# A fused attention, convolution, recurrence and expert layer: who splits the gate weights, and how the recurrence's output tiles are ordered

## What is computed

```python
n = rmsnorm(h, norm1_g) * (1 + sc1) + sh1
(qa, ka, va, u, gb, gc, qc, zf, zb, ic, oc, ga, gbr, gcr) = split(n @ w_in)
o_a = attention(qa, ka, va, cache, rpb)
o_b = gb * conv3(gc * u)
o_c, s_f, s_b = bidirectional_hgrn2(qc, zf, zb, ic, s0)   # f = lb + (1-lb) sigmoid(z)
o_c = rmsnorm_per_head(o_c) * hgrn_g * silu(oc)
mix = (sigmoid(ga) * (o_a @ w_br_a) + sigmoid(gbr) * (o_b @ w_br_b) + sigmoid(gcr) * (o_c @ w_br_c)) @ w_out
h = h + g1 * mix
h = h + g2 * moe(rmsnorm(h, norm2_g) * (1 + sc2) + sh2)   # 64 experts, top 8, and a shared one
y = rmsnorm(h, final_norm_g)
```

## Time and profile before

| | us |
|---|---|
| runs | 1250.66, 1258.70, 1261.13 (median 1258.7) |
| profiled execution, its own time | 1262.51 |
| its span | 1260.7 |
| PE busy | 1144.5 (91%) |
| PEld busy | 700.2 (56%) |
| DVE busy | 446.7 (35%) |
| ACT busy | 291.3 (23%) |
| POOL busy | 180.6 (14%) |

### The profile page before, as it was taken

One profiled execution on the slowest core, in us unless ns is written; L12 is line 12 of the kernel. 1 busy time (PEld: TensorE's weight loads), 2 busy tenths in 40 slices (PEclk: granted clock), 3 DMA queues, 4 the chain that ended last, 5 costly groups with the idle time before them and its releaser, 6 DMA issues.

```text
span 1260.7 us, 14771 instructions
## 1 busy us (share of the span) xinstructions
PE 1144.5 (91%) x4912; PEld 700.2 (56%) x4912; DVE 446.7 (35%) x949; ACT 291.3 (23%) x437; POOL 180.6 (14%) x163
## 2 busy tenths in 40 slices
PE   5999888899888896899987899999999999999965
PEld 2469777687778765556454444444444444444422
DVE  1033333633897835342452221212122121212116
ACT  3124333326434322200131211111111111111001
POOL 0200222000433300000000511112111111111100
PEclk9899898899999997898988999999999999999988
DMA  9845555255633312240046789999999999999464
GB/s 358 258 104 155 81 81 66 76 213 195 224 134 135 134 68 84 68 148 1 1 151 246 282 337 381 386 382 403 379 394 374 382 386 408 391 390 388 171 279 187
DMA packets 86115, 292.40 MB, mean 232 GB/s; under 512 B 10346, under 2 KB 14698, under 8 KB 70954
## 3 DMA queue, kind: packets, MB, share of 16 engines
q1 hardware_dynamic: 69440, 258.05, 53.0%
q0 software_dynamic: 12976, 27.29, 9.6%
q10 hardware_dynamic: 3652, 6.44, 1.5%
HBM read 284.79 MB, written 25.30 MB: 246 GB/s over the span
## 4 chain that ended last, share of the span: by engine, by line
PE 53%; DVE 4%; DMA 4%; ACT 1%; issue 1%; DVEq 0%; SPq 0%; POOL 0%; POOLq 0%
PE PS L1874 14%; PE PS L1530 12%; PE PS L1891 7%; PE PS L1876 7%; PE PS L1893 3%; PE PS L1860 3%; DMA y_parts<-bigB,IDX 2%; PE PS L1540 2%; PE PS L1941 1%; DMA bigA<-in_w_sh_down 1%; DMA nT<-n_rows,IDX 1%; PE PS L1909 1%; PE PS L1740 1%; PE PS L1747 0%; DMA bigA<-y_parts 0%
## 5 line engine op out<-in xcount | busy, mean ns | idle before, releaser
L1581 PE MATMUL PS<-bigB_r 128*128 128x384 f32 x288 | 98.9, 344 | 3.3 <-ACT bigD L743 1.3
L1874 PE MATMUL PS<-bigB 128*128 128x512 f32 x224 | 101.7, 597 | 0.0
L984 POOL DMA_INDIRECT bigB<-n_rows,IDX x29 | 30.0, 1034 | 496.1 <-DVE IDX L1057 249.3
L1583 PE MATMUL PS<-bigB_r,bigA_r 128*128 128x384 f32 x288 | 97.3, 338 | 0.0
L1582 PE MATMUL PS<-nT_r,bigB_r 128*128 128x384 f32 x288 | 97.2, 338 | 0.0
L1874 PE MATMUL PS<-bigA,bigB 128*128 128x512 f32 x208 | 94.9, 599 | 0.0
L1877 PE MATMUL PS<-bigB 128*64 128x512 f32 x208 | 94.8, 599 | 0.0
L1876 PE MATMUL PS<-bigA,bigB 128*64 128x512 f32 x208 | 94.8, 599 | 0.0
L1487 DVE TENSOR_SCALAR bigB<-PS,bigD 128x1024 f32<-128x1024 f32 x40 | 51.4, 1284 | 104.8 <-PE PS L1891 70.6
L1128 DVE TENSOR_TENSOR bigA_r<-bigA,bigB_r 128x2048 fp32r<-128x2048 f32 x18 | 41.3, 2292 | 116.5 <-ACT bigB_r L765 116.5
L907 ACT ACTIVATE bigB<-PS 128x1024 f32<-128x1024 f32 x40 | 41.0, 1024 | 153.3 <-PE PS L1860 149.1
(11 more groups left out here) (336 smaller groups left out, 2003.3 us busy)
## 6 DMA issues: line engine op xcount, KB each, us to landing
bigA<-in_w_in SPq DMA_DIRECT2D x17, 2048.0 KB, 9.1
bigB<-in_w_gate SPq DMA_DIRECT2D x27, 1024.0 KB, 10.5
bigB<-in_w_up SPq DMA_DIRECT2D x27, 1024.0 KB, 13.6
bigB<-in_w_down SPq DMA_DIRECT2D x27, 1024.0 KB
bigA<-in_w_gate SPq DMA_DIRECT2D x26, 1024.0 KB
bigA<-in_w_up SPq DMA_DIRECT2D x26, 1024.0 KB
bigA<-in_w_down SPq DMA_DIRECT2D x26, 1024.0 KB, 11.5
bigA<-in_w_ada SPq DMA_DIRECT2D x8, 2048.0 KB, 9.6
```

The source lines that it names most:

```text
L1581: mm(out, wh, nh, start=(k == 0), stop=False)
L1583: last = mm(out, wl, nh, start=False, stop=(k == KD - 1))
L1874: last = mm(PS[:, 2 + b, :], XT[:, b, k, :], GU_W[s][:, :, k, :], start=first, stop=stop)
```

## The change

GpSimd's low parts of the gate weights go to VectorE (low_part), issued one or two units ahead inside the stages sums and ops, and behind the carry keys for the last ones. All 24 gate units are rounded; n_back and its semaphore are gone. All gate units now stand ahead of carry_t. A new stage late_sig does the first sigmoid and the output gate's SiLU on ScalarE. The output tiles get a bank and a row buffer each (HO_BANK, OS[m]); their stages are split in ho_sq and ho_norm, and branch products 0 to 3 (br) with their gating (brm) are put among them; the other 20 follow. The decayed queries EB are computed in place of the running sums. The modulation rows of the second norm come back as columns, in two transfers (MODP) whose contiguous pieces have eight elements, and VectorE adds them up instead of TensorE's 32 matmuls. The gate bias is added ahead of branch product 8.

The new order of the tail is in the list below (context lines are cut, the indentation of the engine code is reduced by eight):

```diff
 PASSES = UNITS_MAX // BODY
+BR_EARLY = 4
+HO_BANK = (6, 4, 5)
...
-SPLIT_G = [n for n, (name, c, j) in enumerate(UNITS) if name[0] == "g" and name[1].isdigit()][:19]
+SPLIT_G = [n for n, (name, c, j) in enumerate(UNITS) if name[0] == "g" and name[1].isdigit()]
...
         s.append(("split_g", SPLIT_G[SPLIT_G.index(n) + 2]))
-    if n == SPLIT_G[-1]:
-        s.append(("n_back",))
...
     for i in range(16):
-        stages += [(("level", i), 0), (("ops", i + 1) if i < 15 else ("carry",), 1 if i < 15 else 2)]
-    stages += [(("carry_t",), 2), (("carry_products",), 2), (("hout", 0), 1), (("hout_t", 0), 1), (("hout", 1), 1),
-               (("hout_t", 1), 1), (("hout", 2), 1), (("hout_t", 2), 0)]
+        stages += [(("level", i), 0), (("ops", i + 1) if i < 15 else ("carry",), 1 if i < 15 else 5)]
...
         fill = fill[n:]
-    late = [("late_act", b) for b in range(3)]
-    while fill or late:
-        s += late[:1] + sum(fill[:1], [])
-        late, fill = late[1:], fill[1:]
+    assert not fill
+    s += [("carry_t",), ("late_sig",), ("carry_products",), ("br", 0), ("br", 1), ("hout", 0), ("brm", 0), ("brm", 1),
+          ("ho_sq", 0), ("ho_norm", 0), ("hout", 1), ("hout_t", 0), ("ho_sq", 1), ("ho_norm", 1), ("hout", 2), ("br", 2),
+          ("ho_sq", 2), ("ho_norm", 2), ("hout_t", 1), ("br", 3), ("brm", 2), ("hout_t", 2), ("brm", 3)]
+    s += [("late_act", b) for b in range(3)]
...
 XH = cut(bigB, ATT, (NT, D))
-T1 = bigB[:, ATT + 3072:ATT + 3584]
+T1 = OQ = bigB[:, ATT + 3072:ATT + 3584]
...
 GR = bigB[:, 20000:22048]
-Zrows = bigB[:, 22048:24096]
...
 PTC = bigC[:, 5632:5760]
-EB = cut(bigC, 0, (2, HC, 2 * P))
+EB = Z[:, :, :, CTX:T]
 STC = cut(bigC, 2048, (2, HC, P))
-OS, OQ, OR = bigC[:, 3072:3584], bigC[:, 3584:4096], bigC[:, 4096:4608]
+OS = [bigC[:, 3072 + 512 * m:3584 + 512 * m] for m in range(NT)]
+MODP = cut(bigC, 5632, (2, 4, 2 * KD))
...
 nlo_done = sem("n_low_ready")
-nback_done = sem("n_whole_again")
...
+def br_bank(i):
+    return (2, 3, 0, 1)[i % 4] if i < KD else (4, 5, 2, 3, 0, 1)[(i - KD) % 6]
...
             act.wait_ge(b_done, 1)
-            act.wait_ge(nback_done, KD)
             link(nc.scalar.activation(KH, KH, ACT.Exp))
-            nc.scalar.activation(EB, Z[:, :, :, CTX:T], ACT.Exp).then_inc(edec_done, 1)
+            nc.scalar.activation(EB, EB, ACT.Exp).then_inc(edec_done, 1)
...
                                      ACT.Copy).then_inc(kht_taken, 1)
+        elif st == "late_sig":
+            act.wait_ge(unit_taken, len(UNITS))
+            nc.scalar.activation(G[:, 0:8, :], G[:, 0:8, :], ACT.Sigmoid).then_inc(late_done, 1)
+            nc.scalar.activation(OG, OG, ACT.Silu).then_inc(late_done, 1)
...
             act.wait_ge(ho_ready, m + 1)
-            if m > 0:
-                act.wait_ge(ho_norm, m)
-            nc.scalar.activation(OS, PS[:, 6, :], ACT.Copy).then_inc(ho_taken, 1)
+            nc.scalar.activation(OS[m], PS[:, HO_BANK[m], :], ACT.Copy).then_inc(ho_taken, 1)
+            if m == 0:
+                for d in range(2):
+                    act.dma_start(new_state[d].rearrange("h k v -> k h v"), STC[:, d, :, :]).then_inc(state_out, 16)
+        elif st == "ho_norm":
+            m = ev[1]
...
             nc.scalar.activation(small[:, 36:40], small[:, 32:36], ACT.Sqrt).then_inc(ho_root, 1)
-            if m == 0:
-                act.wait_ge(unit_taken, AFTER["oc"])
-                nc.scalar.activation(OG, OG, ACT.Silu).then_inc(late_done, 1)
-                for d in range(2):
-                    act.dma_start(new_state[d].rearrange("h k v -> k h v"), STC[:, d, :, :]).then_inc(state_out, 16)
...
             if b == 0:
-                act.wait_ge(unit_taken, AFTER["g5"])
...
                 for g in range(P // CG):
-                    act.dma_start(bigB[CG * g:CG * g + 2, 20000:24096], ada_rows[g]).then_inc(ada_back, 16)
+                    act.dma_start(GR[CG * g:CG * g + 2, :], ada_rows[g, :, 0:4 * WCH]).then_inc(ada_back, 16)
+                for i in range(2):
+                    cols = ada_rows[:, :, (4 + 2 * i) * WCH:(6 + 2 * i) * WCH].rearrange("g v (p k) -> p (g v) k", k=KD)
+                    act.dma_start(MODP[:, i, :, :].rearrange("p g (v k) -> p (g v) k", v=2), cols).then_inc(ada_back, 16)
...
                 act.dma_start(BG[0:2, :], b_gate).then_inc(bg_loaded, 16)
-            g = G[:, 8 * b:8 * b + 8, :]
-            nc.scalar.activation(g, g, ACT.Sigmoid).then_inc(late_done, 1)
+            else:
+                g = G[:, 8 * b:8 * b + 8, :]
+                nc.scalar.activation(g, g, ACT.Sigmoid).then_inc(late_done, 1)
...
-    for n in SPLIT_G:
-        w, low, i = gate_unit(n)
-        pool.wait_ge(ghi_done, i + 1)
-        nc.gpsimd.tensor_tensor(low, w, GHI[i % 2].bitcast(F32), ALU.subtract).then_inc(glo_done, 1)
...
-    def mod_columns(which, ks, norm, cnt):
+    def mod_columns(which, ks, norm, cnt, src):
...
         n = ks.stop - ks.start
-        src = PS[:, 7, 0:32].rearrange("p (s k v) -> p s v k", s=2, v=2)
...
+    lows = []
...
+    def low_part():
...
+        w, low, i = gate_unit(lows.pop(0))
+        dve.wait_ge(ghi_done, i + 1)
+        nc.vector.tensor_tensor(low, w, GHI[i % 2].bitcast(F32), ALU.subtract).then_inc(glo_done, 1)
...
                 nc.vector.tensor_tensor(NLO[:, k, :], nT[:, k, :], NHI[:, k, :].bitcast(F32), ALU.subtract).then_inc(nlo_done, 1)
-        elif st == "n_back":
-            dve.wait_ge(nlo_done, KD)
-            dve.wait_ge(nmove_done, 1)
-            dve.wait_ge(unit_ready, SPLIT_G[-1] + 1)
-            for k in range(KD):
-                nc.vector.tensor_tensor(nT[:, k, :], NLO[:, k, :].bitcast(F32), NHI2[:, k, :].bitcast(F32), ALU.add).then_inc(nback_done, 1)
+        elif st == "split_g":
+            lows.append(ev[1])
+            if SPLIT_G.index(ev[1]) == 2 or SPLIT_G.index(ev[1]) > 20:
+                low_part()
...
             dve.wait_ge(modt_ready, hf + 1)
-            mod_columns(0, slice(4 * hf, 4 * hf + 4), cc(C_N1), hf + 1)
+            mod_columns(0, slice(4 * hf, 4 * hf + 4), cc(C_N1), hf + 1,
+                        PS[:, 7, 0:32].rearrange("p (s k v) -> p s v k", s=2, v=2))
...
         elif st == "sums":
+            low_part()
...
             for h in range(HC):
+                if h == 2:
+                    low_part()
...
                 take_level(i - 1)
+            else:
+                low_part()
+            low_part()
...
                     ins.then_inc(diff_done, 1)
+            low_part()
...
             dve.wait_ge(in_state, 32)
+            dve.wait_ge(unit_taken, len(UNITS))
...
             nc.vector.tensor_copy(small[:, 83:84], small[:, 56:57]).then_inc(st_done, 1)
-        elif st == "hout":
+        elif st == "ho_sq":
...
             dve.wait_ge(ho_taken, m + 1)
-            link(nc.vector.tensor_tensor(OQ, OS, OS, ALU.mult))
+            link(nc.vector.tensor_tensor(OQ, OS[m], OS[m], ALU.mult))
...
             nc.vector.tensor_scalar(small[:, 32:36], small[:, 40:44], 1.0 / P, EPS, ALU.mult, ALU.add).then_inc(ho_ms, 1)
+        elif st == "ho_norm":
+            m = ev[1]
...
             rsqrt_fix(small[:, 32:36], small[:, 36:40], small[:, 44:48], small[:, 88:92])
-            if m > 0:
-                dve.wait_ge(hot_ready, m)
-            nc.vector.tensor_tensor(OR.rearrange("p (h v) -> p h v", h=HC), OS.rearrange("p (h v) -> p h v", h=HC),
-                                    small[:, 44:48].unsqueeze(2).broadcast_to([P, HC, P]), ALU.mult).then_inc(ho_norm, 1)
+            rows = OS[m].rearrange("p (h v) -> p h v", h=HC)
+            nc.vector.tensor_tensor(rows, rows, small[:, 44:48].unsqueeze(2).broadcast_to([P, HC, P]), ALU.mult).then_inc(ho_norm, 1)
+            dve.wait_ge(ho_norm, m + 1)
+        elif st == "brm":
+            i = ev[1]
+            dve.wait_ge(late_done, 1)
+            dve.wait_ge(br_ready, i + 1)
+            nc.vector.tensor_tensor(G[:, i, :], PS[:, br_bank(i), 0:T], G[:, i, :], ALU.mult).then_inc(br_taken, 1)
...
             m = ev[1]
-            dve.wait_ge(late_done, 1)
+            dve.wait_ge(late_done, 2)
...
-            dve.wait_ge(unit_taken, len(UNITS))
-            dve.wait_ge(bg_loaded, 16)
-            dve.wait_ge(ada_back, 64)
-            nc.vector.tensor_tensor(GR[0:2, :], GR[0:2, :], BG[0:2, :], ALU.add).then_inc(gr_ready, 1)
-            for i in range(24):
+            for i in range(BR_EARLY, 24):
                 br, j = i // KD, i % KD
+                if i == KD:
+                    dve.wait_ge(bg_loaded, 16)
+                    dve.wait_ge(ada_back, 96)
+                    nc.vector.tensor_tensor(GR[0:2, :], GR[0:2, :], BG[0:2, :], ALU.add).then_inc(gr_ready, 1)
...
                     dve.wait_ge(late_done, 2 + br)
+                    dve.wait_ge(br_taken, i)
...
                 g = G[:, 8 * br + j, :]
-                nc.vector.tensor_tensor(g, PS[:, i % 6, 0:T], g, ALU.mult).then_inc(br_taken, 1)
```

(46 more changed lines are left out.)

## The result

The changed kernel takes **1220.0 us** (median of four runs, 1213.4 to 1221.3) where the kernel before takes 1254.8 on the same chip: a ratio of **0.971, 95% interval 0.965 to 0.977**. The profiled execution of after has a span of 1219.4 us and a time of 1221.25, for 1260.7 and 1262.51 before.

A forecast was written before the change was run, and what follows sets the result against it. VectorE, standing still behind GpSimd, was taken to pace the level steps. 12.4 - 3.7 + 10.2 + 13.4 + 9.1 = 41.4, less 2 allowance, gave 1223.1 us for the profiled execution, 1219 for the median; range 1209 to 1238.

The forecast's parts named there:

- The allowance of 2 us: TensorE idling 2.6 us ahead of the first transposes might halve its clock, costing 3 to 5; 2 us put in.
- The level steps: Low parts on VectorE: round 6.2 us instead of 7.59, level 15 at 433.7 instead of 446.07; gain 12.4 us.
- The five rounded units: Units 19 to 23 behind level 15, before the carry products: stage takes 29.0 us for 25.3; loss 3.7.
- Carry products to the first tile: VectorE's path from carry products to first output tile unchanged at 9.0 us; nothing gained, tile starts at 471.7.
- The 1.7 us that the prediction worked out by that rule: ScalarE before the first output tile: 1.38 us drain beside each table load would add some 1.7 us to the sum.
- The output tiles: Three tiles overlapped in the new order: 18.3 us for 28.5; gain 10.2, bounds 6 and 12.
- Branch products and gate rows: Behind the tiles: 20 branch products instead of 24 gain 13.4 us; modulation columns on VectorE and gate rows gain 9.1.
- The rival of late modulation rows: Two new transfers of 1024 32-byte pieces land late, stopping VectorE at branch product 8; 1271 us at 78 us, chance 0.03.
- the rival it belongs to: Half clock returns: idles at 475 and 487 drop TensorE's clock over tiles and branch products; 1225 us, chance 0.22.
- the 673.5 us behind: The stretch from the first output product (587.2) to the end is not touched by the change.

The follow-up runs named there:

- low_pool: The changed kernel with the low parts of all 24 rounded gate units subtracted on GpSimd again; median 1234.5 us, ratio 0.977 to the kernel before.
- low_only: The kernel before with only its 19 low parts moved to VectorE between the level steps; median 1243.0 us, ratio 0.986 to the kernel before.
- low_twice: The changed kernel with each low part of the level steps subtracted a second time on VectorE into a scratch; median 1233.9 us, ratio 0.978.
- eb_later: The changed kernel with the exponential of the output decays issued two rounded units later on ScalarE; median 1222.4 us, ratio 0.969.
- unround5: The changed kernel with the last five gate units unrounded again after re-adding the activations, all ahead of the carry transposes; median 1222.8 us, ratio 0.966.
- tiles_serial: The changed kernel with the three output tiles one after the other again, branch products 2 and 3 behind the last; median 1235.9 us, ratio 0.979.
- mod_pe: The changed kernel with the modulation columns made by 32 small TensorE products as before; median 1226.5 us, ratio 0.971.
- tiles_later: The changed kernel with a branch product ahead of each group of transposes and two more products moved in; median 1216.7 us, ratio 0.966.
- both_later: The changed kernel with the later output-decay exponential and branch products 2 to 5 among the output tiles; median 1208.9 us, ratio 0.961.
- before_again: The kernel before, unchanged, run for a second profile; one run, 1269.2 us.

## Why the prediction was right

The forecast was 1219 us; the median is 1220.0. The mechanism was right. That the number agrees within 1 us is luck: the steps of the sum gave 45.7 us where it had 41.4, and 39.4 after the allowance; nearly all of that error has one sign, and it was made up for behind the first output product (7). The median of before was 1258.7 when the forecast was made and 1254.8 with the fourth run, so the medians differ by 34.8 us only.

1. **The level steps** gained 14.8 where I had 12.4. The mechanism stands (low_pool, low_only, low_twice). The round was 5.96 for my 6.2: I took the overlap of successive instructions off the differences alone (1.9), and durations for the masks and the low part (1.06 and 1.2), while the rows have 0.96 and 1.13 from start to start. Twelve steps by 0.24 are 2.9, most of the error. The steps with an adaLN unit went as foreseen: one of them and the step behind it take 13.35 us for 13.5.
2. **The five rounded units** lost 2.8 where I had 3.7. I had the waits at 1.2 and 2.1, on units 20 and 21; they were 0.93 and 1.99. The second was there for a cause that I named (two exponentials) but took as given, and eb_later took it away. The rest of the error is behind the units, where transposes and copies took 2.3 for 2.9. Rounding these five is worth 2.0 (unround5).
3. **Carry products to the first tile** took 9.05, as foreseen, with two table loads on ScalarE. This is its timeline there:

```profile
459.08 1.08 ACT L828 ACTIVATE bigB<-PS 128x512 f32<-128x512 f32 x2 [0.32 <-PE PS L1715]
460.18 1.28 ACT L832 ACT_TABLE_LOAD   x1
461.48 2.76 ACT L832 ACTIVATE bigB<-bigB 128x3072 f32<-128x3072 f32 x1
464.26 1.28 ACT L833 ACT_TABLE_LOAD   x1
465.55 1.49 ACT L833 ACTIVATE bigD<-bigD 128x1536 f32<-128x1536 f32 x1
```

Each load of 1.28 us starts within 0.02 of the end of the activation ahead of it, and the next activation starts 0.02 behind. The Trainium skill, ScalarE: Activation LUTs, What ACT_TABLE_LOAD costs, adds about 1.38 us of drain to each switch; no such gap is in these rows, nor in the earlier trace rows, and the measurement decides. The 1.7 us that the prediction worked out by that rule did not come; by its own terms, 464 and 6.8 us and two drains, ScalarE would also have come 0.8 late to the copy, not 0.3.
4. **The output tiles** gained 11.3 (17.24 for 28.5) where I had 10.2. tiles_serial shows that the order brings this: without it TensorE idles 4.4 us three times and its clock falls three times, as before.
5. **Branch products and gate rows** gained 22.3 (12.5 and 9.8) where I had 22.5. From the last transposes to the gate rows 52.97 us passed; I had 52.4. The gate rows took 3.67 of TensorE at full clock for 6.26, and the first output product came 3.5 behind their start. The rival of late modulation rows did not come up: VectorE added the gate bias at 496.66 without a wait, 13.7 us after the first of the two new transfers was issued, and mod_pe shows the small products to have been worth 8.5.
6. **The allowance of 2 us** for a fall of the clock was not needed in this profile. But the rival it belongs to is real. Of the kernels with overlapping tiles that kept both idles, after, after_again, low_pool, low_twice and mod_pe had no fall at the last transposes; unround5 and eb_later had one, at 1.7 us each; low_twice had one in the carry stage. I had priced that rival, with two long falls, at 6 us; one fall of 3.4 us cost 1.7.
7. **What failed is the sentence that the 673.5 us behind are not touched.** As a statement on the work it is right. As a number it was one draw: C was 677.7 in this profile, 4.3 more, with 49 us of half clock for 36. With C unchanged this execution would have been 6 us below the 1223.1 of my sum, not 2.

## What to carry to other kernels

Before moving work to a third engine, look at the slowest instance beside the median of its neighbour's instruction: 2765 ns beside 548 was worth about 14 us of 1255 here, while the engine that caused it was idle most of the time. Build a pipelined round from start to start, not from durations. Where an engine's share is computed from one profile, take a second profile of the same kernel first: here the untouched half moved by 6 us with the clock, more than unround5, eb_later or tiles_later changed.

## What the runs showed of the hardware beyond that

- **The length of an idle time did not decide on the clock.** An idle of 2.08 or 2.09 us ahead of the same transposes left TensorE at 2.4 GHz in after and dropped it to 1.2 GHz in unround5 and eb_later, each time for 3.4 us. In the carry stage the idle of 1.99 us left it full in after, and one of 1.98 us dropped it in low_twice, from 454.9 to 458.3. Idles of 4.4 us dropped it all three times (tiles_serial), and one of 5.09 us for 6.8 us (low_pool). A gain of 2.0 us ahead of such a place (eb_later) can vanish in it, and filling the idle (both_later) keeps it.
- **The scatter between runs goes with the clock.** The seven runs of before beside low_pool have spans from 1249.1 at a mean clock of 0.965 to 1263.9 at 0.952. The part ahead of the levels moves as well: level 0 starts at 326.5 in low_only, with 17 us of half clock ahead of it, and at 338.9 in before_again, with 42.
- **The clock fell with no idle at all** among 32 small products that took 7.5 us without a gap (mod_pe; before has 0.62 over the same stage).
